# Two-layer hybrid step in split float32: three 256-column matmuls into one PSUM half instead of a 512- and a 256-column one

## The chip, the cores and the metric

The kernel runs on one core of a Trainium2 chip. The metric is the device time of one execution in microseconds; the median of several executions is compared. The engines are PE (TensorE, with its weight loads shown apart as PEld), DVE (VectorE), ACT (ScalarE), POOL (GpSimd) and SP (SyncE, which here only issues DMAs).

## The reference, cut to what matters

Two layers are computed for 128 context tokens and 128 latent tokens, 256 tokens in all. Nearly all of the arithmetic is in five products of a token matrix with a weight matrix, in each layer:

```
h = rms_norm(x, g_attn) * (1 + scale1) + shift1
proj = h @ w_in                                  # 2048 -> 3584
...                                              # conv module, two attentions -> concat
x = x + gate1 * (concat @ w_out)                 # 2048 -> 2048
h2 = rms_norm(x, g_mlp) * (1 + scale2) + shift2
x = x + gate2 * (square(relu(h2 @ w_mlp1)) @ w_mlp2)   # 2048 -> 8192 -> 2048
```

The modulation vectors (shift, scale, gate) come from a sixth product, silu(c) @ w_ada with 2048 x 12288 weights, for two vectors only. All inputs are float32, and nothing may be computed in a coarser format.

## The kernel before, in words

Tokens lie in the free dimension (256 columns, TOK), features in the partitions. Every weight matrix is walked in **pairs**: a pair is a strip of 512 output columns by 2048 rows, loaded by SP as four 1 MB blocks into `raw`. A layer has 2 + 3 + 2 pairs of w_in (kinds in1, in2, in3), 4 of w_out (out), and four chunks of 4 pairs of w_mlp1 (up) and 4 of w_mlp2 (down). That makes 43 pairs in a layer and 86 in the kernel.

To keep float32's accuracy each operand is split into two parts. ACT rounds a raw block into `hi` (L596) and DVE computes `lo` = raw - hi (L786), 1024 elements per partition at a time. The activations are kept split as well: `hs` (the normalized input) and `act2` (the mixer's output, or the hidden layer) hold for each of 16 feature tiles 512 columns, first the 256 of the high part and behind them the 256 of the low part. The product that is wanted is hi x high + hi x low + lo x high.

A pair has two groups g, and a group has 2 output tiles j with one PSUM bank each (banks 0 to 3 in all) and 16 steps k over the input features. For each (k, j), called a weight tile here, PE before the change issues two matmuls: L442 multiplies the hi tile with all 512 columns of the activations into the whole bank, so hi x high lands in the left half and hi x low in the right one, and L444 adds lo x high (256 columns) into the right half. There are 86 x 2 x 16 x 2 = 5504 weight tiles. Each matmul comes with a weight load of its own on PEld.

The two halves of a bank are added when it is read. ACT copies the right half into `tmp` (L642). DVE then adds left half and tmp. For in1 to in3 that sum goes to `zc` or `zq` (L839). For the others it goes to `tsum` (L842), and from there up squares the positive part (L845), and out and down add gate x sum to the residual `xT`, once for each stream of 128 tokens (L851). The semaphore `bank_freed` counts these adds, and PE waits for it before it starts on a bank again and at the start of attention. For out and down ACT squares the new residual (L653) and DVE adds it to `ssq` (L867), whose column sum PE needs for the next norm (L457).

Between the groups' own work DVE also does the 31 taps of the convolution (L884, 12 instructions behind each group of in2 and in3) and, in in3, the norms of queries and keys (reciprocals L921, product L927). PE does the modulation products (L380, L397) in between, as jobs of 4 units in a pair. Each engine takes its instructions in the written order: `walk` calls each engine's `pair` and `stage` in the same order, and the engines meet by semaphores only.

## Time and profile before

| | us |
|---|---|
| three timed executions | 2500.26, 2513.34, 2516.66 |
| their median | 2513.34 |
| span of the profiled execution, first to last instruction | 2495.1 |

The profiled execution has no time of its own beside its span. Its span lies 18.2 us under the median of the timed runs and 5.2 us under the fastest of them; what a timed execution has around the span is in that difference. Sums below are made on the span and moved to the median by adding 18.2. PE is the engine with the longest busy time.

### The profile page before, as it was taken

The page shows a single profiled execution, that of the slowest core. Times are in us where ns is not written, and L with a number is a line of the kernel's source. Part 1 is how long each engine was busy: PE and PEld are TensorE (multiplying, and loading weights), DVE is VectorE, ACT ScalarE, POOL GpSimd, SP SyncE. Part 2 cuts the span into 40 slices and gives each one's busy share as a digit, 9 for nine tenths or more (in the row PEclk, how much of TensorE's full clock was granted, in tenths as well). Part 3 has the DMA queues.
Part 4 walks back from the last instruction along what each step waited for, and adds up shares of the span by engine and source line. Part 5 has one row for each costly group of instructions (what it writes and reads, how often), then busy time and mean ns, then how long its engine had stood idle before and what let it go on. Part 6 is the DMA issues. An engine that isn't in the chain of part 4 may idle for free.

```text
span 2495.1 us, 41360 instructions
## 1 busy us (share of the span) xinstructions
PE 2326.7 (93%) x13464; PEld 1843.4 (74%) x13464; DVE 1541.3 (62%) x2642; ACT 1082.7 (43%) x1699; POOL 144.5 (6%) x196
## 2 busy tenths in 40 slices
PE   6699888979999999999997998797999999999997
PEld 2277556757887887787785775586778888888886
DVE  1357775574665565565567577867556666666666
ACT  1243334444444444444444333344444544545543
POOL 3101000001000001000100110000000000000000
PEclk9699899989999999999998998998999999999999
DMA  9878655858668768758854886444865655655662
GB/s 380 330 284 307 218 189 188 303 203 299 229 211 297 248 197 290 281 191 274 307 184 153 293 308 210 150 137 150 279 243 195 185 192 189 186 197 180 190 200 87
DMA packets 415092, 569.71 MB, mean 228 GB/s; under 512 B 9604, under 2 KB 364472, under 8 KB 414776
## 3 DMA queue, kind: packets, MB, share of 16 engines
q1 hardware_dynamic: 360504, 365.50, 44.8%
q0 software_dynamic: 52224, 201.34, 21.5%
q10 hardware_dynamic: 2304, 2.10, 0.2%
q8 instruction: 34, 0.56, 0.1%
q14 instruction: 26, 0.21, 0.0%
HBM read 565.76 MB, written 3.15 MB: 228 GB/s over the span
## 4 chain that ended last, share of the span: by engine, by line
PE 85%; DVE 6%; DMA 3%; ACT 2%; issue 2%; DVEq 1%; SPq 0%; ACTq 0%; POOL 0%; POOLq 0%
PE bank L442 51%; PE bank L444 25%; PE bank L380 6%; DMA ada<-in_w_ada 3%; PE bank L397 1%; DVE qrs L921 1%; DVE yconv L884 1%; PE bank L457 1%; DMA vrows<-in_g_final 1%; DVE lo L786 1%; DVE ybuf L1025 1%; DVE hs L1033 1%; DVEq L1033 0%; ACT prob L734 0%; ACT hs L754 0%
## 5 line engine op out<-in xcount | busy, mean ns | idle before, releaser
L442 PE MATMUL bank<-hs,hi 128*128 128x512 f32 x2944 | 1072.1, 407 | 49.0 <-DVE hs L1033 37.9
L786 DVE TENSOR_TENSOR lo<-raw,hi 128x1024 fp32r<-128x1024 f32 x685 | 816.9, 1223 | 453.6 <-ACT hi L596 453.2
L596 ACT ACTIVATE hi<-raw 128x1024 fp32r<-128x1024 f32 x685 | 704.0, 1055 | 575.0 <-PE bank L444 569.1
L442 PE MATMUL bank<-act,hi 128*128 128x512 f32 x2560 | 895.8, 396 | 6.0 <-DVE act L973 6.0
L444 PE MATMUL bank<-hs,lo 128*128 128x256 f32 x2944 | 827.4, 281 | 0.0
L442 PEld LDWEIGHTS bank<-hs,hi 128*128 128x128 f32 x2944 | 560.5, 190 | 295.4 <-issue 146.0
L444 PE MATMUL bank<-act,lo 128*128 128x256 f32 x2560 | 711.3, 278 | 0.0
L442 PEld LDWEIGHTS bank<-act,hi 128*128 128x128 f32 x2560 | 481.9, 188 | 131.2 <-issue 19.8
L444 PEld LDWEIGHTS bank<-hs,lo 128*128 128x128 f32 x2944 | 562.3, 191 | 1.4 <-issue 1.4
L444 PEld LDWEIGHTS bank<-act,lo 128*128 128x128 f32 x2560 | 482.6, 189 | 0.0
L642 ACT ACTIVATE tmp<-bank 128x256 f32<-128x256 f32 x344 | 113.4, 382 | 381.0 <-PE bank L444 381.0
L842 DVE TENSOR_TENSOR tsum<-bank,tmp 128x256 f32<-128x256 f32 x288 | 121.4, 422 | 200.0 <-ACT tmp L642 200.0
L349 POOL DMA_DIRECT2D ada<-in_w_ada x160 | 120.2, 751 | 1639.6 <-PE bank L380 1609.3
L380 PE MATMUL bank<-ada,cT 128*32 128x512 f32 x1344 | 184.7, 623 | 10.0 <-DMA ada<-in_w_ada 9.9
L653 ACT ACTIVATE thid<-xT 128x256 f32 (+1 forms) x160 | 67.1, 419 | 165.8 <-DVE xT L851 164.6
L851 DVE SCALAR_TENSOR_TENSOR xT<-tsum,mods,xT 128x128 f32 (+1 forms) x320 | 98.4, 349 | 43.1 <-DVE tsum L842 42.9
L884 DVE SCALAR_TENSOR_TENSOR yconv<-hpad,vecs,yconv 128x256 f32<-128x256 f32 x240 | 96.6, 479 | 0.0
L867 DVE TENSOR_TENSOR ssq<-ssq,thid 128x256 f32<-128x256 f32 x160 | 67.7, 423 | 31.4 <-ACT thid L653 31.2
L647 ACT ACTIVATE act<-thid 128x256 f32 x128 | 53.8, 420 | 73.7 <-DVE thid L845 73.7
L380 PEld LDWEIGHTS bank<-ada,cT 128*32 128x32 f32 x1344 | 27.0, 109 | 59.8 <-issue 40.2
L859 DVE TENSOR_TENSOR act<-thid,act 128x256 f32 x128 | 54.5, 426 | 25.9 <-ACT act L647 24.4
L397 PEld LDWEIGHTS bank<-cst,rows 128*128 128x128 f32 x384 | 52.9, 211 | 19.1 <-ACT rows L602 15.2
(127 smaller groups left out, 818.6 us busy)
## 6 DMA issues: line engine op xcount, KB each, us to landing
raw<-in_w_mlp SPq DMA_DIRECT2D x256, 1024.0 KB, 6.2
ada<-in_w_ada POOLq DMA_DIRECT2D x168, 1024.0 KB, 6.9
raw<-in_w_in SPq DMA_DIRECT2D x56, 1024.0 KB, 6.3
raw<-in_w_out SPq DMA_DIRECT2D x32, 1024.0 KB, 6.0
pre_a<-in_w_ada POOLq DMA_DIRECT2D x16, 1024.0 KB, 16.9
pre_q<-in_w_ada POOLq DMA_DIRECT2D x8, 1024.0 KB, 19.0
xtok<-in_x_prompt SPq DMA_DIRECT2D x1, 1024.0 KB, 11.9
xtok<-in_x_sample SPq DMA_DIRECT2D x1, 1024.0 KB, 21.3
```

Source lines behind the costliest of these rows:

```text
L349: pool.dma_start(ada[:, s % 2, :, :], src[:, 4 * s:4 * s + 4, bass.ds(b * 512, 512)]).then_inc(ada_landed[s % 2], 16)
L380: mm = pe.matmul(ada_ps[32 * q:32 * q + 32, :], cT[:, 4 * s + q, :], unit[:, q, :], start=(s == 0), stop=(s == 3))
L397: mm = pe.matmul(mod_ps[:, 2 * q:2 * q + 2], rows[:, q * P:(q + 1) * P], sel, start=True, stop=True)
L442: pe.matmul(bank[:, :], hi[:, h, k, j * P:(j + 1) * P], acts[:, k_, :], start=(k_ == 0), stop=False)
L444: mm = pe.matmul(bank[:, TOK:2 * TOK], lo[:, h, k, j * P:(j + 1) * P], acts[:, k_, 0:TOK], start=False, stop=(k_ == KT - 1))
L596: act.activation(hi[:, o % 4, :, :], raw[:, (o // 2) % 4, 4 * (o % 2):4 * (o % 2) + 4, :], ACT.Copy).then_inc(hi_ready, 1)
L642: act.activation(tmp[:, j, :], pb[2 * g + j][:, TOK:2 * TOK], ACT.Copy)\
L786: dve.tensor_tensor(lo[:, o % 4, :, :], raw[:, (o // 2) % 4, 4 * (o % 2):4 * (o % 2) + 4, :], hi[:, o % 4, :, :].bitcast(f32), ALU.subtrac ...
L842: dve.tensor_tensor(tsum[:, j, :], bank, tmp[:, j, :], ALU.add).then_inc(bank_freed, 1)
L851: dve.scalar_tensor_tensor(x, tsum[:, j:j + 1, s * P:(s + 1) * P], mods[:, l, bass.ds(gate + 4 * i + 2 * g + j, 1), s], x, ALU.mult, ALU.a ...
L867: dve.tensor_tensor(ssq[:, :], ssq[:, :], thid[:, j, :], ALU.add)\
L884: dve.scalar_tensor_tensor(y, hpad[:, ch, :, bass.ds(tap, P)], vecs[:, l, 1, bass.ds(4 * tap + ch, 1)], y, ALU.mult, ALU.add).then_inc(con ...
```

## The change: three matmuls per weight tile, and one half to read

The left half of the bank takes all three products, 256 columns each: hi x high, hi x low, lo x high. The number of columns that stream through PE for a weight tile stays 768. The number of matmuls and of weight loads goes from two to three, since the hi tile is named twice. Nothing is left in the right half.

The bank is then complete in one place. For in1 to in3 ACT copies it straight to `zc` or `zq`, and DVE has no part in it. For up ACT applies the relu on the way to `tmp` and DVE squares that. For out and down DVE reads the bank directly in the residual update and ACT has no part in it. `tsum` goes, and `bank_freed` and `x_updated` are replaced by three semaphores (`z_freed`, `hid_freed`, `res_freed`), each counted by the engine that reads. So that their counts can be constants, the loops over the out pairs and over the first chunk's up pairs are written out in the program, where they were loops on the engines' sequencers.

```diff
-                        after(pe, bank_freed, 4 * n + 2 * g - 2)
+                        if kind in ("out", "down"):
+                            after(pe, res_freed, res_tiles(l, c) + 4 * i + 2 * g - 2)
+                        if kind == "down":
+                            pe.wait_ge(hid_freed, up_tiles(l, c) + KT + 2 * g - 2)
+                        elif kind == "up":
+                            after(pe, hid_freed, up_tiles(l, c) + 4 * i + 2 * g - 2)
+                            pe.wait_ge(res_freed, res_tiles(l, c) + 2 * g - 2)
+                        elif kind != "out":
+                            after(pe, z_freed, in_tiles(l, kind) + 4 * (i - IN2 * (kind == "in3")) + 2 * g - 2)
...
-                                    pe.matmul(bank[:, :], hi[:, h, k, j * P:(j + 1) * P], acts[:, k_, :],
+                                    pe.matmul(bank[:, 0:TOK], hi[:, h, k, j * P:(j + 1) * P], acts[:, k_, 0:TOK],
                                               start=(k_ == 0), stop=False)
-                                    mm = pe.matmul(bank[:, TOK:2 * TOK], lo[:, h, k, j * P:(j + 1) * P],
+                                    pe.matmul(bank[:, 0:TOK], hi[:, h, k, j * P:(j + 1) * P], acts[:, k_, TOK:2 * TOK],
+                                              start=False, stop=False)
+                                    mm = pe.matmul(bank[:, 0:TOK], lo[:, h, k, j * P:(j + 1) * P],
                                                    acts[:, k_, 0:TOK], start=False, stop=(k_ == KT - 1))
...
                         for j in range(2):
-                            after(act, bank_freed, 4 * n + 2 * g + j - 1)
-                            act.activation(tmp[:, j, :], pb[2 * g + j][:, TOK:2 * TOK], ACT.Copy)\
-                               .then_inc(tmp_ready, 1)
+                            bank = pb[2 * g + j][:, 0:TOK]
+                            if kind in ("in1", "in2", "in3"):
+                                z = zc if kind == "in1" else zq
+                                act.activation(z[:, bass.ds(4 * i + 2 * g + j, 1), :], bank.unsqueeze(1), ACT.Copy)\
+                                   .then_inc(z_freed, 1)
+                            elif kind == "up":
+                                act.activation(tmp[:, j, :], bank, ACT.Relu).then_inc(hid_freed, 1)
...
-                            dve.wait_ge(tmp_ready, done)
-                            if kind in ("in1", "in2", "in3"):
-                                z = zc if kind == "in1" else zq
-                                dve.tensor_tensor(z[:, tile, :], bank.unsqueeze(1), tmp[:, j:j + 1, :], ALU.add)\
-                                   .then_inc(bank_freed, 1)
-                                continue
-                            dve.tensor_tensor(tsum[:, j, :], bank, tmp[:, j, :], ALU.add).then_inc(bank_freed, 1)
-                            dve.wait_ge(bank_freed, done)
+                            bank = pb[2 * g + j]
                             if kind == "up":
-                                dve.scalar_tensor_tensor(thid[:, j, :], tsum[:, j, :], 0.0, tsum[:, j, :],
-                                                         ALU.max, ALU.mult).then_inc(relu2_ready, 1)
-                            else:
+                                dve.wait_ge(hid_freed, up_tiles(l, c) + 4 * i + 2 * g + j + 1)
+                                dve.tensor_tensor(thid[:, j, :], tmp[:, j, :], tmp[:, j, :], ALU.mult)\
+                                   .then_inc(relu2_ready, 1)
+                            elif kind in ("out", "down"):
+                                dve.wait_ge(half_used, 8 * n + 4 * g + 4)
                                 gate = GATE1 if kind == "out" else GATE2
                                 for s in range(S):
                                     x = xT[:, tile, s * P:(s + 1) * P]
-                                    dve.scalar_tensor_tensor(
-                                        x, tsum[:, j:j + 1, s * P:(s + 1) * P],
+                                    update = dve.scalar_tensor_tensor(
+                                        x, bank[:, s * P:(s + 1) * P].unsqueeze(1),
                                         mods[:, l, bass.ds(gate + 4 * i + 2 * g + j, 1), s], x,
-                                        ALU.mult, ALU.add).then_inc(x_updated, 1)
+                                        ALU.mult, ALU.add)
+                                update.then_inc(res_freed, 1)
```

On PE the first pair of layer 0 (in1) begins like this before, in the program's order; hs, hi and lo are the operands named above:

```order
L457 MATMUL bank7<-ssq_65,ones_64 128x256 [waits ssq_set]
L442 MATMUL bank0<-hs_50,hi_53 128x512 [waits hs_ready,lo_ready]
L444 MATMUL bank0<-hs_50,lo_54 128x256
```

and like this after:

```order
L466 MATMUL bank7<-ssq_64,ones_63 128x256 [waits ssq_set]
L449 MATMUL bank0<-hs_50,hi_53 128x256 [waits hs_ready,lo_ready]
L451 MATMUL bank0<-hs_50,hi_53 128x256
L453 MATMUL bank0<-hs_50,lo_54 128x256
L449 MATMUL bank1<-hs_50,hi_53 128x256
```

One matmul has become two with the same weight tile, and all of a weight tile's three go to the same columns.

On DVE the first pair of in3 (layer 0) stands like this before:

```order
L786 TENSOR_TENSOR lo<-raw,hi 128x1024 [waits hi_ready] x4
L839 TENSOR_TENSOR zq<-bank,tmp 128x256 [waits tmp_ready] x2
L884 SCALAR_TENSOR_TENSOR yconv<-hpad,vecs,yconv 128x256 [waits conv_tap] x12
L921 RECIPROCAL qrs<-qrs 128x512 [waits qstd_ready] x2
```

and like this after:

```order
L799 TENSOR_TENSOR lo<-raw,hi 128x1024 [waits hi_ready] x4
L891 SCALAR_TENSOR_TENSOR yconv<-hpad,vecs,yconv 128x256 [waits conv_tap] x12
L928 RECIPROCAL qrs<-qrs 128x512 [waits qstd_ready] x2
```

The two adds between the splits and the convolution taps are gone, and with them DVE's wait for ACT's copy of the group that PE is still working on.

At the end of a group of out pairs DVE does this before:

```order
L842 TENSOR_TENSOR tsum<-bank,tmp 128x256 [waits tmp_ready]
L851 ISA [waits bank_freed]
L851 ISA
L851 SCALAR_TENSOR_TENSOR xT<-tsum,mods,xT 128x128
```

and this after:

```order
L857 SCALAR_TENSOR_TENSOR xT<-bank,mods,xT 128x128 [waits half_used]
L857 SCALAR_TENSOR_TENSOR xT<-bank,mods,xT 128x128
```

The update now waits for PE alone, and neither ACT's copy nor the sum stands ahead of it.

## Rows read from the trace of the kernel before

**Rows 1.** The page: span, and each engine's busy time, share and instructions.
```profile
span 2495.1 us, 41360 instructions
PE 2326.7 (93%) x13464; PEld 1843.4 (74%) x13464; DVE 1541.3 (62%) x2642; ACT 1082.7 (43%) x1699; POOL 144.5 (6%) x196
```

**Rows 2.** The page: the chain that ended last, by engine and by line.
```profile
PE 85%; DVE 6%; DMA 3%; ACT 2%; issue 2%; DVEq 1%; SPq 0%; ACTq 0%; POOL 0%; POOLq 0%
PE bank L442 51%; PE bank L444 25%; PE bank L380 6%; DMA ada<-in_w_ada 3%; PE bank L397 1%; DVE qrs L921 1%; DVE yconv L884 1%; PE bank L457 1%; DMA vrows<-in_g_final 1%; DVE lo L786 1%; DVE ybuf L1025 1%; DVE hs L1033 1%; DVEq L1033 0%; ACT prob L734 0%; ACT hs L754 0%
```

**Rows 3.** Busy time by windows: stretch, busy PE, PEld, DVE, ACT, POOL (instructions), clock, DMA.
```profile
1750.00:2475.00 725.00, 724.35 (x4192) 620.83 (x4192) 465.78 (x701) 349.10 (x507) 9.02 (x12) 1.00 0.60 197
```

**Rows 4.** Timeline of PE at full clock, out pair of layer 0: start, duration, instruction.
```profile
499.83 0.39 PE L442 MATMUL bank<-act,hi 128*128 128x512 f32 x1
500.06 0.27 PE L444 MATMUL bank<-act,lo 128*128 128x256 f32 x1
500.17 0.40 PE L442 MATMUL bank<-act,hi 128*128 128x512 f32 x1
...
500.52 0.39 PE L442 MATMUL bank<-act,hi 128*128 128x512 f32 x1
...
502.60 0.39 PE L442 MATMUL bank<-act,hi 128*128 128x512 f32 x1
```

**Rows 5.** Timeline of PEld, the same stretch.
```profile
500.06 0.19 PEld L442 LDWEIGHTS bank<-act,hi 128*128 128x128 f32 x1
500.17 0.19 PEld L444 LDWEIGHTS bank<-act,lo 128*128 128x128 f32 x1
```

**Rows 6.** The chain in order of time: eight matmuls summing in one bank, eight 2-column ones.
```profile
342.17 1.98 PE bank L457 x8
...
452.04 0.79 PE bank L397 x8
```

**Rows 7.** Timeline of PE at half clock (0.50), behind the third norm.
```profile
1347.00 0.63 PE L442 MATMUL bank<-hs,hi 128*128 128x512 f32 x1
1347.43 0.41 PE L444 MATMUL bank<-hs,lo 128*128 128x256 f32 x1
1347.64 0.63 PE L442 MATMUL bank<-hs,hi 128*128 128x512 f32 x1
```

**Rows 8.** Timeline of DVE in the first in3 pair, layer 0; brackets: idle before, and its releaser.
```profile
273.07 1.23 DVE L786 TENSOR_TENSOR lo<-raw,hi 128x1024 fp32r<-128x1024 f32 x1 [3.32 <-ACT hi L596]
276.87 0.76 DVE L839 TENSOR_TENSOR zq<-bank,tmp 128x256 f32<-128x256 f32 x2 [2.57 <-ACT tmp L642]
277.54 4.83 DVE L884 SCALAR_TENSOR_TENSOR yconv<-hpad,vecs,yconv 128x256 f32<-128x256 f32 x12
282.29 6.56 DVE L921 RECIPROCAL qrs<-qrs 128x512 f32<-128x512 f32 x2
288.76 4.56 DVE L786 TENSOR_TENSOR lo<-raw,hi 128x1024 fp32r<-128x1024 f32 x4
```

**Rows 9.** Timeline of ACT and PE, what that stretch waits for and holds up.
```profile
288.74 1.06 ACT L596 ACTIVATE hi<-raw 128x1024 fp32r<-128x1024 f32 x1 [2.19 <-PE bank L444]
...
302.37 2.08 PE L485 MATMUL bank<-zq,cst 128*128 128x512 f32 x2 [9.30 <-DVE zq L927]
```

**Rows 10.** Timeline of DVE at the entry of attention, layer 0.
```profile
330.20 4.62 DVE L786 TENSOR_TENSOR lo<-raw,hi 128x1024 fp32r<-128x1024 f32 x4
...
337.11 4.83 DVE L884 SCALAR_TENSOR_TENSOR yconv<-hpad,vecs,yconv 128x256 f32<-128x256 f32 x12
```

**Rows 11.** Timeline of ACT, DVE and PE at the end of the out pairs, layer 0.
```profile
508.29 0.66 ACT L642 ACTIVATE tmp<-bank 128x256 f32<-128x256 f32 x2 [2.48 <-PE bank L444]
509.39 0.61 DVE L851 SCALAR_TENSOR_TENSOR xT<-tsum,mods,xT 128x128 f32 x2 [0.26 <-DVE tsum L842]
511.79 0.43 DVE L867 TENSOR_TENSOR ssq<-ssq,thid 128x256 f32<-128x256 f32 x1 [0.24 <-ACT thid L653]
512.27 1.22 PE L457 MATMUL bank<-ssq,ones 128*128 128x256 f32 x2 [3.31 <-DVE ssq L867]
```

More of the change, by code:

```diff
@@ L48 @@
 PAIRS = DEPTH * PAIRS_LAYER
+Z_LAYER = 4 * (IN1 + IN2 + IN3)
 BANKS = 6 * D // 512
@@ L118, in build @@
     tmp = place("tmp", [P, 2, TOK], f32)
-    tsum = place("tsum", [P, 2, TOK], f32)
     thid = place("thid", [P, 2, TOK], f32)
@@ L194, in build @@
     half_used = sem("half_used")
-    tmp_ready = sem("tmp_ready")
-    bank_freed = sem("bank_freed")
+    z_freed, hid_freed, res_freed = sem("z_freed"), sem("hid_freed"), sem("res_freed")
     hs_ready = sem("hs_ready")
@@ L246, in walk @@
         stage("clear", -1)
-        with eng.Fori(0, OUT) as i:
+        for i in range(OUT):
             pair("out", n + i, i, -1, a + 16 + i if first else None, False)
@@ L250, in walk @@
         n += OUT
-        with eng.Fori(0, UP) as i:
+        for i in range(UP):
             pair("up", n + i, i, 0, a + 20 + i, False)
@@ L489, in attention @@
                     a = l * BANKS + (15 if l == 0 else 19)
-                    pe.wait_ge(bank_freed, 4 * (l * PAIRS_LAYER + IN1 + IN2 + IN3))
+                    pe.wait_ge(z_freed, Z_LAYER * (l + 1))
                     exchange(QW, 0)
@@ L650, in pair @@
                                 r = res_tiles(l, c) + 4 * i + 2 * g + j
-                                act.wait_ge(x_updated, 2 * r + 2)
+                                act.wait_ge(res_freed, r + 1)
                                 act.wait_ge(ssq_steps, ssq_base(l, c) + 4 * i + 2 * g + j)
@@ L669, in qk_norms @@
                         act.dma_start(ktokc[:, KV:2 * KV, :], t["cache_win_k"][0, l]).then_inc(cache_landed[0], 16)
-                        act.wait_ge(bank_freed, 4 * (l * PAIRS_LAYER + IN1 + IN2))
+                        act.wait_ge(z_freed, in_tiles(l, "in3"))
                         squares(l, 0)
@@ L764, in stage @@
                     elif name == "gate":
-                        act.wait_ge(bank_freed, 4 * (l * PAIRS_LAYER + IN1))
+                        act.wait_ge(z_freed, in_tiles(l, "in2"))
                         act.activation(zc[:, CT:2 * CT, :], zc[:, CT:2 * CT, :], ACT.Sigmoid)\
@@ L833, in pair @@
                             tile = bass.ds(4 * i + 2 * g + j, 1)
-                            done = 4 * n + 2 * g + j + 1
-                            bank = pb[2 * g + j][:, 0:TOK]
-                            dve.wait_ge(tmp_ready, done)
-                            if kind in ("in1", "in2", "in3"):
-                                z = zc if kind == "in1" else zq
-                                dve.tensor_tensor(z[:, tile, :], bank.unsqueeze(1), tmp[:, j:j + 1, :], ALU.add)\
-                                   .then_inc(bank_freed, 1)
-                                continue
-                            dve.tensor_tensor(tsum[:, j, :], bank, tmp[:, j, :], ALU.add).then_inc(bank_freed, 1)
-                            dve.wait_ge(bank_freed, done)
-                            if kind == "up":
-                                dve.scalar_tensor_tensor(thid[:, j, :], tsum[:, j, :], 0.0, tsum[:, j, :],
-                                                         ALU.max, ALU.mult).then_inc(relu2_ready, 1)
-                            else:
+                            bank = pb[2 * g + j]
+                            if kind == "up":
+                                dve.wait_ge(hid_freed, up_tiles(l, c) + 4 * i + 2 * g + j + 1)
[3 more added lines that the diff above has]
+                                dve.wait_ge(half_used, 8 * n + 4 * g + 4)
                                 gate = GATE1 if kind == "out" else GATE2
@@ L1077, in exps_before, with in_tiles @@
     return 5 * HEADS * l + 2 * min(e, HEADS) + 3 * max(0, e - HEADS)
+def in_tiles(l, kind):
+    return Z_LAYER * l + 4 * {"in1": 0, "in2": IN1, "in3": IN1 + IN2}[kind]
 def up_tiles(l, c):
```

2 lines of the change are left out of this document (1 added, 1 removed).

## The prediction

> **What bounds the kernel now.** I read the page first. PE is busy for 93% of the span, DVE for 62%, ACT for 43% [rows 1]. Busy shares of PE are modelled, so the chain of waits comes next: it runs on PE for 85% of the span, and 51% + 25% = 76% of the span lies on the two matmuls that the change touches, L442 and L444 [rows 2]. DVE has 6% of the chain, mostly around norms and attention. The windows say the same: in the up and down pairs of layer 1 PE is busy for 724.35 of 725.00 us at full clock [rows 3]. A cheaper evacuation on DVE or ACT gains nothing there. What counts is the time that PE takes for one weight tile, times 5504.
>
> That time is read from starts, since durations of successive matmuls overlap. In a steady stretch at full clock L442 starts at 499.83 and, eight weight tiles later, at 502.60 [rows 4]: 2.77 / 8 = 0.346 us for a weight tile. Within one, L444 starts 0.23 behind L442 (500.06 - 499.83), and the next L442 0.11 behind L444 (500.17 - 500.06). Over the eight tiles the second distance reads 0.11 or 0.12 alternately, so 0.115, and the first is what remains, 0.231. In columns that is 0.231 / 512 = 0.451 ns and 0.115 / 256 = 0.449 ns. Both shapes stream at the same price per column, with nothing left over for an instruction. At half clock a pair is 0.43 + 0.21 = 0.64 us for 768 columns [rows 7], again proportional, 0.83 ns per column.
>
> **The change, part by part.** (1) *Three matmuls for two, same columns.* The hi x high part is now 256 columns, hi x low 256 more, lo x high 256 as before. The row nearest to each of the three is L444 itself: a 256-column matmul with the next tile's 128-column load underneath, 0.115. So 3 x 0.115 = 0.345 against 0.346, which is -0.001 to -0.002 us for a tile; with -0.0015 x 5504 I take **-8 us**. The bounds come from the same rows. Below: all three at the lower reading, 3 x 0.1125 = 0.3375 (0.1125 because the view shows hundredths and reads 0.11), so -0.0085 x 5504 = -47 us. Above, first: all three at the higher reading, 3 x 0.1175 = 0.3525, so +0.0065 x 5504 = +36 us. The higher reading stands where the next matmul takes another row of the activations (k changes), and after the change the activations' address moves at nearly every matmul. Above, farther: see rival C.
>
> (2) *The third weight load.* A load has to fit under the matmul ahead of it. L442's load starts with L444 (500.06 both), L444's load with L442 (500.17 both) [rows 4, 5], and the matmul that uses L442's load starts 0.11 later, so a load needs at most 0.11 although its row says 0.19. That loads can follow each other at that rate is shown by the eight matmuls with only two moving columns each: 0.79 us, 0.10 each, or 0.11 if it is taken as seven distances [rows 6]. Loads are then 3 x 0.10 to 0.11 = 0.30 to 0.34 us of a tile's 0.345: hidden, with almost no room. Contention that lengthened a load would show at once, where today half of the loads have 0.23 us of cover. That counts for the upper side of the range. PEld's busy share would rise from 74% by about half, to some 110%; that is an artefact of overlapping records.
>
> The Trainium skill speaks against the change here: "TensorE: Matmul & The Clock Gate", The mechanism (Part 3), has weight loads overlap matmuls in flight only where the row groups differ, which they don't. By it each extra load, 0.10 us by the rows, would be exposed, 5504 x 0.10 = +550 us, time about 3050. The trace disagrees: the loads of rows 5 run under matmuls that use the same rows of the array. I give it 1 in 100. The same page, Back-to-back issue gap, adds a constant of about 2.5 ns to each warm matmul; by that one more matmul per tile would be 5504 x 2.5 ns = +14 us, an estimate. The rows show no constant, but can't exclude one so small.
>
> (3) *Adding to the same columns three times running.* Today the right half is written by two matmuls running. Eight matmuls of 256 columns into one bank's same columns take 1.98 us at attention's start, 0.25 each [rows 6]; these are slower plain float32 products, so it shows only that no large wait exists. I take zero, and the bound is the +36 above.
>
> (4) *Evacuation.* In steady pairs it lies beside PE and is worth nothing either way: a bank is wanted again a whole group, some 11 us, later (32 x 0.345). It counts where PE waits for DVE at the end. Three kinds of places:
>
> In in3 PE waits 9.30 us for the norms of queries and keys [rows 9], in each layer. DVE comes late to it because, behind its splits (end 273.07 + 1.23 = 274.30), it idles 2.57 us for ACT's tmp and adds for 0.76 before the taps can start at 277.54 [rows 8]. After the change the taps start at 274.3, the reciprocals end at 285.6 instead of 288.76, and the four splits follow. The last of these is then held by ACT's hi of 288.74 + 1.06 = 289.80 [rows 9], so it ends at 291.0 rather than 293.32: **2.3 us** are left of 3.2. Twice: 4.6.
>
> At the entry of attention the splits end at 330.20 + 4.62 = 334.82, yet the last taps start at 337.11 [rows 10] and PE's sum over the convolution follows them at 342.17 [rows 6]. Now nothing stands between: 2.3 us, twice, 4.6.
>
> At the end of out (two layers) and of the last down (two) the path is PE, tmp, tsum, xT, tsum, xT, thid, ssq, PE, from 508.29 to 512.27 = 3.98 us [rows 11]. After it, four updates at about 0.3 (0.61 for two), then square and add as before (0.43 each, with 0.1 between): 1.2 + 1.0 = 2.2. That is 1.8 less, four times: 7.2. It supposes that DVE reads PSUM in this operation as fast as SBUF.
>
> Together **-16 us**. If half of each turned into another wait it would be -8; nothing makes it a loss. ACT does the same number of reads or fewer, and its one new duty (zq itself) ends where tmp did.
>
> (5) *New waits and code.* PE's waits on z_freed, hid_freed and res_freed ask for reads a group back, long done. Behind a late one the whole PE stream would queue; I count zero. The out pairs and four up pairs of a layer are now straight code, and PE's program is longer; in3 is straight code already and its PE rows keep the pace between the waits. Zero, up to +10.
>
> **Sum.** 2495.1 - 8 - 16 = 2471 for the span, and with the 18.2 us between span and median 2489. That is 1.0% under 2513. A change under 1% either way can't be told from none in this kernel, whose three runs lie 0.65% apart.
>
> **The rivals.**
> A, *load-bound and faster*. The 512-column matmul has an excess of its own (0.231 against 0.213 for 512 columns at 2.4 GHz), and 256-column ones fall to the floor of the load, 0.1125. For it: half of the distances read 0.11 today. Against: the alternate ones read 0.12. -47 - 16 = -63: 2450.
> B, *each change of the activations' address costs*. 0.1175 for all three: +36 - 16 = +20: 2533. For it: the alternation of 0.11 and 0.12 goes with k. Against: 0.231 for 512 columns is twice 0.115, not twice 0.1175.
> C, *the excess belongs to the hi tile's matmul, not to its columns*; this is the case on the slow side. L442 takes 0.231 where 512 columns at 2.4 GHz are 0.213: 0.018 over. If that is a price of each matmul with a long-row hi operand, there are now two per tile: 2 x (0.107 + 0.018) + 0.115 = 0.365, +0.019 x 5504 = +105, less 16: 2602. It decides from an excess of 5 ns per tile up (5504 x 5 ns = 28 us, more than 16 + 8 together). For it: the excess is there at full clock and not at half clock, where 0.43 is 512 columns at 1.2 GHz. Against: per column both shapes agree to 0.5%.
> D, *the change doesn't do what it says*: a repeated load of the same tile is left out by the build. Then loads have more cover; columns still set the pace, and the time is the forecast's.
>
> **How the numbers follow.** Forecast with D 0.46 (2470 to 2505 by its own parts), A 0.20, B 0.18, C 0.13, anything else (exposed loads, new stalls) 0.03. The range 2448 to 2545 holds the forecast, A and B with the small constants, 0.84, and leaves out C. Faster by over 1% means under 2488: A whole and nearly half of the forecast's, 0.41. Within 1%: the rest of the forecast's and most of B, 0.42. Slower: C, a little of B, the rest, 0.17.
>
> **What the changed profile would show.** In a steady stretch, three matmul starts per tile at 0.11 to 0.12 and 0.345 in sum (0.3375 would be A, 0.3525 B, 0.365 C). PEld starts with each of them. PE's wait in in3 at about 7 us instead of 9.30; taps directly behind the splits there; 2.2 instead of 3.98 us from the last group to L457's successor. I am wrong if the tile's time is off by over 5 ns in either direction, since nothing else is multiplied by 5504.

## The result, and the profile after

| | before | after |
|---|---|---|
| median of four executions, us | 2514.04 | 2535.79 |
| their range | 2500.26 to 2516.66 | 2535.72 to 2537.56 |
| span of the profiled execution | 2495.1 | 2534.2 |

The ratio, taken over all executions of both, is 1.0098, with a 95% interval from 1.0067 to 1.0128: the change makes the kernel 1.0% slower. The medians lie 21.8 us apart, which is 0.9%. The forecast was 2489, a kernel faster by 1.0%. The measured time lies inside the stated range of 2448 to 2545, but the step went the other way. The profiled execution after took 2535.85 with a span of 2534.2, so only 1.65 us lie around a span. The executions before spread over 16 us, those after over 2 us; the profiled one before was a quick one, so the two spans lie 39.1 us apart where the medians lie 21.8 apart.

The page after, first the engines, then the chain of waits (to be compared with [rows 1, 2]):

```profile
span 2534.2 us, 50390 instructions
PE 2385.2 (94%) x18968; PEld 2162.0 (85%) x18968; DVE 1416.2 (56%) x2298; ACT 1036.3 (41%) x1539; POOL 144.5 (6%) x196
...
PE 87%; DVE 4%; DMA 3%; ACT 2%; issue 1%; DVEq 1%; SPq 0%; ACTq 0%; POOL 0%; POOLq 0%
PE bank L449 27%; PE bank L451 26%; PE bank L453 26%; PE bank L379 6%; DMA ada<-in_w_ada 3%; PE bank L396 1%; PE bank L466 1%; DVE hs L1040 1%; DMA vrows<-in_g_final 1%; DVE ybuf L1032 1%; DVE qrs L928 1%; DVEq L1040 0%; PE bank L494 0%; ACT prob L747 0%; SPq L311 0%
```

PE has 5504 more matmuls, DVE and ACT 344 and 160 fewer instructions. DVE's share of the chain fell from 6% to 4%, as an evacuation that got out of the way would make it. PE's share rose: 79% of a longer span lie on the three matmuls, 76% before. So the loss is to be looked for in the stream itself.

The timeline of PE in a steady stretch at full clock, up pair of layer 1 (start, duration, instruction), answers to [rows 4]:

```profile
1999.75 0.28 PE L449 MATMUL bank<-hs,hi 128*128 128x256 f32 x1
1999.87 0.28 PE L451 MATMUL bank<-hs,hi 128*128 128x256 f32 x1
1999.99 0.28 PE L453 MATMUL bank<-hs,lo 128*128 128x256 f32 x1
2000.11 0.28 PE L449 MATMUL bank<-hs,hi 128*128 128x256 f32 x1
...
2000.83 0.28 PE L449 MATMUL bank<-hs,hi 128*128 128x256 f32 x1
```

The durations of neighbours overlap, so the distances between starts are read. From 1999.75 to 2000.83 there are three weight tiles: 0.360 us for one, and each of the three matmuls takes 0.120. Before it was 0.346. The distance doesn't alternate any more, whether the activations' row changes or not. The windows say the same of a long stretch of layer 1 (columns as in [rows 3], which it answers to): 6023 / 3 = 2008 tiles in 725.00 us are 0.361 for one, where 4192 / 2 = 2096 were 0.346.

```profile
1780.00:2505.00 725.00, 725.00 (x6023) 713.00 (x6020) 406.75 (x561) 323.36 (x434) 8.27 (x11) 1.00 0.61 191
```

The loads start with the matmuls, 0.120 apart, by PEld's timeline (answers to [rows 5]):

```profile
1999.87 0.19 PEld L453 LDWEIGHTS bank<-hs,lo 128*128 128x128 f32 x1
1999.99 0.19 PEld L449 LDWEIGHTS bank<-hs,hi 128*128 128x128 f32 x1
2000.11 0.19 PEld L451 LDWEIGHTS bank<-hs,hi 128*128 128x128 f32 x1
```

At half clock, behind the third norm (window 1366.5 to 1369, granted clock 0.55 with its end at full), PE's timeline reads like this (answers to [rows 7]):

```profile
1366.35 0.41 PE L449 MATMUL bank<-hs,hi 128*128 128x256 f32 x1
1366.56 0.41 PE L451 MATMUL bank<-hs,hi 128*128 128x256 f32 x1
1366.78 0.41 PE L453 MATMUL bank<-hs,lo 128*128 128x256 f32 x1
1366.99 0.41 PE L449 MATMUL bank<-hs,hi 128*128 128x256 f32 x1
```

A tile takes 0.64 us there, exactly what two matmuls took before. 768 columns at 1.2 GHz are 0.640. So the third matmul costs 13.5 ns at full clock and nothing at half clock.

In sums over the whole trace: the distances from one matmul of a weight tile to the next such matmul (those under 0.7 us, so without waits) are 1934.9 us before and 1994.3 after, +59.4. This is called the stream below. All the rest, from PE's first start to its last, goes from 547.7 to 527.6, -20.1. Together that is +39.3, where the spans differ by 39.1. A tile at full clock takes 348.1 ns in the mean before and 359.8 after (some before run slower than 346.5, see experiment 8), and 11.7 ns for some 5040 of them is 59.

The second term is the evacuation, and it came as forecast. DVE, then PE, in the first in3 pair of layer 0 (answers to [rows 8, 9]):

```profile
275.66 1.23 DVE L799 TENSOR_TENSOR lo<-raw,hi 128x1024 fp32r<-128x1024 f32 x1 [3.35 <-ACT hi L605]
276.80 4.83 DVE L891 SCALAR_TENSOR_TENSOR yconv<-hpad,vecs,yconv 128x256 f32<-128x256 f32 x12
281.55 6.56 DVE L928 RECIPROCAL qrs<-qrs 128x512 f32<-128x512 f32 x2
288.02 3.43 DVE L799 TENSOR_TENSOR lo<-raw,hi 128x1024 fp32r<-128x1024 f32 x3
292.60 1.23 DVE L799 TENSOR_TENSOR lo<-raw,hi 128x1024 fp32r<-128x1024 f32 x1 [1.15 <-ACT hi L605]
```
```profile
302.88 2.08 PE L494 MATMUL bank<-zq,cst 128*128 128x512 f32 x2 [7.40 <-DVE zq L934]
```

The taps follow the split with nothing between, and PE waits 7.40 us instead of 9.30. The fourth split behind the reciprocals waits 1.15 us for ACT's hi, as the prediction supposed, and for longer. At attention's entry the splits end at 335.67, the taps run directly behind them, and PE's sum over yconv starts at 340.65 without a wait (answers to [rows 10]):

```profile
335.59 4.84 DVE L891 SCALAR_TENSOR_TENSOR yconv<-hpad,vecs,yconv 128x256 f32<-128x256 f32 x12
```
```profile
340.65 1.97 PE L466 MATMUL bank<-yconv,ones 128*128 128x256 f32 x8
```

And at the end of out, layer 0, four updates in 1.13 us, then the squares, and PE's wait is 1.40 instead of 3.31 (answers to [rows 11]):

```profile
510.15 1.13 DVE L857 SCALAR_TENSOR_TENSOR xT<-bank,mods,xT 128x128 f32<-128x128 f32 x4 [1.69 <-PE bank L453]
511.29 0.95 DVE L874 TENSOR_TENSOR ssq<-ssq,thid 128x256 f32<-128x256 f32 x2
```
```profile
512.30 0.70 PE L466 MATMUL bank<-ssq,ones 128*128 128x256 f32 x2 [1.40 <-DVE ssq L874]
```

### The profile page after: what moved, and what is told of

Same layout as the page of the kernel before. It is cut to its first block, busy times and chain, and to the rows that moved or that the text cites. A ratio compares the mean times of both kernels' runs of the same rounds, so it can differ in the third digit from the quotient of the medians.

```text
span 2534.2 us, 50390 instructions
## 1 busy us (share of the span) xinstructions
PE 2385.2 (94%) x18968; PEld 2162.0 (85%) x18968; DVE 1416.2 (56%) x2298; ACT 1036.3 (41%) x1539; POOL 144.5 (6%) x196
## 4 chain that ended last, share of the span: by engine, by line
PE 87%; DVE 4%; DMA 3%; ACT 2%; issue 1%; DVEq 1%; SPq 0%; ACTq 0%; POOL 0%; POOLq 0%
PE bank L449 27%; PE bank L451 26%; PE bank L453 26%; PE bank L379 6%; DMA ada<-in_w_ada 3%; PE bank L396 1%; PE bank L466 1%; DVE hs L1040 1%; DMA vrows<-in_g_final 1%; DVE ybuf L1032 1%; DVE qrs L928 1%; DVEq L1040 0%; PE bank L494 0%; ACT prob L747 0%; SPq L311 0%
## 5 line engine op out<-in xcount | busy, mean ns | idle before, releaser
L799 DVE TENSOR_TENSOR lo<-raw,hi 128x1024 fp32r<-128x1024 f32 x685 | 830.2, 1224 | 736.0 <-ACT hi L605 734.4
L605 ACT ACTIVATE hi<-raw 128x1024 fp32r<-128x1024 f32 x685 | 717.1, 1057 | 802.7 <-PE bank L453 795.3
L449 PE MATMUL bank<-hs,hi 128*128 128x256 f32 x2944 | 859.0, 292 | 46.0 <-DVE hs L1040 36.2
L451 PE MATMUL bank<-hs,hi 128*128 128x256 f32 x2944 | 838.7, 285 | 0.0
L449 PE MATMUL bank<-act,hi 128*128 128x256 f32 x2560 | 728.8, 285 | 5.4 <-DVE act L980 5.4
L451 PE MATMUL bank<-act,hi 128*128 128x256 f32 x2560 | 726.0, 284 | 0.0
L453 PE MATMUL bank<-act,lo 128*128 128x256 f32 x2560 | 725.9, 284 | 0.0
L449 PEld LDWEIGHTS bank<-hs,hi 128*128 128x128 f32 x2944 | 570.0, 194 | 164.4 <-issue 126.6
L451 PEld LDWEIGHTS bank<-hs,hi 128*128 128x128 f32 x2944 | 570.9, 194 | 1.4 <-issue 1.4
L449 PEld LDWEIGHTS bank<-act,hi 128*128 128x128 f32 x2560 | 493.0, 193 | 19.2 <-issue 10.9
L451 PEld LDWEIGHTS bank<-act,hi 128*128 128x128 f32 x2560 | 493.2, 193 | 0.0
L857 DVE SCALAR_TENSOR_TENSOR xT<-bank,mods,xT 128x128 f32 (+1 forms) x320 | 90.3, 345 | 75.8 <-PE bank L453 75.7
L850 DVE TENSOR_TENSOR thid<-tmp 128x256 f32<-128x256 f32 x128 | 48.8, 423 | 105.5 <-ACT tmp L656 105.4
L656 ACT ACTIVATE tmp<-bank 128x256 f32<-128x256 f32 x128 | 42.3, 383 | 151.1 <-PE bank L453 151.1
```

The costliest lines, as they stand in the source:

```text
L449: pe.matmul(bank[:, 0:TOK], hi[:, h, k, j * P:(j + 1) * P], acts[:, k_, 0:TOK], start=(k_ == 0), stop=False)
L451: pe.matmul(bank[:, 0:TOK], hi[:, h, k, j * P:(j + 1) * P], acts[:, k_, TOK:2 * TOK], start=False, stop=False)
L453: mm = pe.matmul(bank[:, 0:TOK], lo[:, h, k, j * P:(j + 1) * P], acts[:, k_, 0:TOK], start=False, stop=(k_ == KT - 1))
L605: act.activation(hi[:, o % 4, :, :], raw[:, (o // 2) % 4, 4 * (o % 2):4 * (o % 2) + 4, :], ACT.Copy).then_inc(hi_ready, 1)
L799: dve.tensor_tensor(lo[:, o % 4, :, :], raw[:, (o // 2) % 4, 4 * (o % 2):4 * (o % 2) + 4, :], hi[:, o % 4, :, :].bitcast(f32), ALU.subtrac ...
L850: dve.tensor_tensor(thid[:, j, :], tmp[:, j, :], tmp[:, j, :], ALU.mult)\
```

## The experiments

Each time is compared with executions of the kernel before that were measured beside it; their medians were 2517.42 (experiments 1 to 4), 2516.66 (5 and 8 to 10), 2517.18 (6, 7 and 11) and 2511.12 (12). The profile of the kernel before has a span of 2495.1, well under these. Experiments 2 to 8 with one execution each have no interval; they are there for their traces.

**The theory (P):** at full clock every matmul, with its own 128-column weight load, costs about 13 ns over its columns. Two made 320 + 26.5 = 346.5 ns before, three make 320 + 40 = 360. **The rivals:** (S) three products into the same PSUM columns hold each other up; (L) 0.120 is the time that a weight load needs, so that 256 columns no longer cover it; (R) it is a rate at which columns are taken, and more columns cost more of it; naming the same weight tile twice, or the order of the three, costs something; and, for the sum, that the evacuation lost time rather than gained it.

**1. Two halves.** The kernel before with L442 cut in two, each part into its own half. Evacuation as before.

```diff
-pe.matmul(bank[:, :], hi[...], acts[:, k_, :], start=(k_ == 0), stop=False)
+pe.matmul(bank[:, 0:TOK], hi[...], acts[:, k_, 0:TOK], start=(k_ == 0), stop=False)
+pe.matmul(bank[:, TOK:2 * TOK], hi[...], acts[:, k_, TOK:2 * TOK], start=False, stop=False)
```

> The kernel before, with only its 512-column matmul cut into two of 256 columns that write the two halves of the bank as before: three matmuls and three weight loads per weight tile, but evacuation, semaphores and loops of before. Theory P (a price of some 13 ns per matmul with its load, on top of its columns): 0.360 us per weight tile, as after the change, and a time some 58 us over the kernel before. Theory S (adding to the same 256 columns three times running is what costs): 0.346 us and no change. My prediction's cost per column alone: 0.346 and no change.

Measured 2553.36 (2553.07 to 2554.93); ratio to before 1.0145, interval 1.0128 to 1.0162. Timeline of PE:

```profile
1999.74 0.28 PE L442 MATMUL bank<-hs,hi 128*128 128x256 f32 x1
1999.86 0.28 PE L444 MATMUL bank<-hs,hi 128*128 128x256 f32 x1
1999.98 0.28 PE L446 MATMUL bank<-hs,lo 128*128 128x256 f32 x1
2000.10 0.28 PE L442 MATMUL bank<-hs,hi 128*128 128x256 f32 x1
```

Also 0.120 each and 0.360 for a tile, and the stream takes 1994.7 us where the change's takes 1994.3. Two halves or one makes no difference: S is out. The whole loss is there with the matmuls alone. What the change gets back by everything else, the evacuation above all, is 2553.36 - 2535.79 = 17.6 us; in the traces the rest of PE's time is 545.2 us here and 527.6 after the change, also 17.6. The expected 58 us came in the stream (+59.8 over the first profile), but in time the kernel is only 36 us over the executions beside it; experiment 8 shows why that can be.

**2. The lo matmul widened to 512 columns.** Still two matmuls, now 1024 columns; it adds lo x low, which isn't wanted.

```diff
-mm = pe.matmul(bank[:, TOK:2 * TOK], lo[...], acts[:, k_, 0:TOK], ...)
+mm = pe.matmul(bank[:, :], lo[...], acts[:, k_, :], ...)
```

> The kernel before, with the lo tile's matmul widened to all 512 columns (lo x high into the left half, lo x low into the right one, a term more than wanted): two matmuls, two loads, 1024 columns per weight tile. Theory P: 1024 columns at 2.4 GHz are 426.7 ns, plus 2 x 13.3 = 453 ns per weight tile, time about +590 us. Theory R (the price is one per column, 0.451 ns or 0.469 ns, and something shifts it from the lower to the higher): 462 or 480 ns, +636 or +735 us.

Measured 3061.24 in one execution, span 3059.5. Timeline of PE:

```profile
1999.63 0.39 PE L442 MATMUL bank<-act,hi 128*128 128x512 f32 x1
1999.85 0.39 PE L444 MATMUL bank<-act,lo 128*128 128x512 f32 x1
2000.08 0.39 PE L442 MATMUL bank<-act,hi 128*128 128x512 f32 x1
...
2000.99 0.39 PE L442 MATMUL bank<-act,hi 128*128 128x512 f32 x1
```

Three tiles in 1.36 us, 0.453 each: 1024 columns at 2.4 GHz are 426.7 ns, and 2 x 13.2 on top. In time it is 544 us over the 2517.42 beside it, less than the 590 that P had and farther from R's 636; the tile is what tells them apart. A price per column would give 1024 x 0.451 = 462 ns, and at the change's 0.120 for 256 columns 480: R is out. The price sits on the matmul (with its load), for 256 columns as for 512. L can't be the whole story either: under a matmul of 0.2265 us a load of 0.120 would not show, and the same 13 ns are there.

**3 and 4. Half of the lo load, and its control.** In both, the order is hi x high, lo x high, hi x low, so that the same hi tile is not named twice running; in 3 the lo matmul has 64 of its 128 weight columns and fills half of the output rows.

```diff
-pe.matmul(bank[:, 0:TOK], hi[...], acts[:, k_, TOK:2 * TOK], start=False, stop=False)
-mm = pe.matmul(bank[:, 0:TOK], lo[:, h, k, j * P:(j + 1) * P], acts[:, k_, 0:TOK], ...)
+pe.matmul(bank[0:64, 0:TOK], lo[:, h, k, j * P:j * P + 64], acts[:, k_, 0:TOK], ...)
+mm = pe.matmul(bank[:, 0:TOK], hi[...], acts[:, k_, TOK:2 * TOK], ...)
```

> The changed kernel with the order hi x high, lo x high, hi x low, and with the lo tile's load and matmul cut to 64 of 128 weight columns (the lo correction is left out for half of the outputs; the 256 streamed columns stay). Beside it e4_order has the same order with whole loads. Theory L (a load takes 0.120 us in this stream and 256 columns no longer cover it): the distance under which the halved load lies falls to 0.107 to 0.113, the other two stay at 0.120, some -0.01 per weight tile and -50 us. Theory P or R: all three stay at 0.120. If the price of 13 ns belongs to the load and goes with its columns: one distance 0.113.

> The changed kernel with the three matmuls in the order hi x high, lo x high, hi x low, so that no two neighbours use the same weight tile. Theory P, R and L: 0.360 us per weight tile and the changed kernel's time, 2536. If naming the same tile twice running had a price of its own: less than 0.360.

The control (all 128 columns) took 2537.53 with a span of 2535.9, 0.120 for each matmul and 0.360 for a tile:

```profile
1999.80 0.28 PE L453 MATMUL bank<-hs,hi 128*128 128x256 f32 x1
...
2000.16 0.28 PE L453 MATMUL bank<-hs,hi 128*128 128x256 f32 x1
```

So order and naming a tile twice cost nothing, and a repeated load isn't left out. With half of the lo load it is 2486.04, span 2484.3:

```profile
1999.76 0.28 PE L453 MATMUL bank<-hs,hi 128*128 128x256 f32 x1
1999.88 0.28 PE L449 MATMUL bank<-hs,hi 128*128 128x256 f32 x1
2000.00 0.28 PE L451 MATMUL bank<-hs,lo 128*64 128x256 f32 x1
2000.11 0.28 PE L453 MATMUL bank<-hs,hi 128*128 128x256 f32 x1
...
2001.16 0.28 PE L453 MATMUL bank<-hs,hi 128*128 128x256 f32 x1
```

Four tiles in 1.40, 0.350 each, so 10 ns of the 40 went with half a load: 51.5 us of 2537.5. No matmul lost a column of moving data. So in this form the excess goes with the weights (their load, or how many columns of the array they fill), not with the number of instructions alone. P as written down before the run had no change here and missed; L had the 50 us. A price in proportion to the width of the load would have given 6.7 ns, half of 13.3, so that isn't it either. The three distances read 116, 115 and 119 ns over the trace, where the expectation had all of them or two of them at 0.120; but distances between unequal neighbours don't say which matmul gained. This experiment alone does not exclude L.

**5. The lo matmul with 128 moving columns.** It leaves out the lo correction for the latent tokens. Its 53 ns of columns can't cover the load of the matmul behind it, so this shows what a load takes.

```diff
-mm = pe.matmul(bank[:, 0:TOK], lo[...], acts[:, k_, 0:TOK], ...)
+mm = pe.matmul(bank[:, 0:P], lo[...], acts[:, k_, 0:P], ...)
```

> The changed kernel with the lo tile's matmul cut to 128 of 256 columns (the lo correction is left out for the latent tokens), whole loads. Theory P with no floor under it: 640 columns at 2.4 GHz and 3 x 13.3 = 307 ns per weight tile, time about 2240. Theory P with a load's own time of 0.112 us (the 2-column matmuls) as floor: the distance behind the short matmul is 0.112, the tile 0.352, time about 2492. Theory L (a load takes 0.120 in this stream): that distance stays 0.120, the tile 0.360, time 2536.

Measured 2475.95, span 2474.2. A matmul that waits for its weights is recorded early here (0.33 instead of 0.28 long), so the loads are read. PEld:

```profile
1999.99 0.19 PEld L449 LDWEIGHTS bank<-hs,hi 128*128 128x128 f32 x1
2000.10 0.19 PEld L451 LDWEIGHTS bank<-hs,hi 128*128 128x128 f32 x1
2000.22 0.19 PEld L453 LDWEIGHTS bank<-hs,lo 128*128 128x128 f32 x1
2000.34 0.19 PEld L449 LDWEIGHTS bank<-hs,hi 128*128 128x128 f32 x1
```

L449's load starts with the short lo matmul, and the next load follows 0.11 later (0.108 to 0.112 over the trace); the two other distances are 0.116 to 0.125. So a load can be done in 0.11 in this stream. Together with experiment 2 that speaks against L: the 0.120 of the change is not a load laid bare, since a load would fit with 8 ns or more to spare. A tile takes 345 to 352 ns, 349 in the mean, against 352 expected by P with the load as a floor; the time is 16 us under the 2492 that went with it.

**6. Half of the rows.** The order of experiments 3 and 4, and the lo matmul with 64 of its 128 rows, to tell the load's columns from its rows (the line of hi x low moves behind it, not shown).

```diff
+pe.matmul(bank[:, 0:TOK], lo[0:64, h, k, j * P:(j + 1) * P], acts[0:64, k_, 0:TOK], ...)
```

> As e3_half_lo_load, but the lo tile is cut to 64 of its 128 rows (half of the contraction of lo x high is left out), with all 128 weight columns. If the price goes with weight columns: 0.360 per weight tile, 2537. If it goes with the amount loaded or with the rows in use: 0.350 and about 2486.

Measured 7466.22: nothing of the sort that was expected. PE, then PEld (the bracket is idle time before):

```profile
1999.79 0.41 PE L449 MATMUL bank<-hs,hi 128*128 128x256 f32 x1
2000.13 0.58 PE L451 MATMUL bank<-hs,lo 64*128 64x256 f32 x1
2000.64 0.58 PE L453 MATMUL bank<-hs,hi 128*128 128x256 f32 x1
2001.02 0.41 PE L449 MATMUL bank<-hs,hi 128*128 128x256 f32 x1
```
```profile
2000.13 0.28 PEld L451 LDWEIGHTS bank<-hs,lo 64*128 64x128 f32 x1 [0.22 <-issue]
2000.64 0.29 PEld L453 LDWEIGHTS bank<-hs,hi 128*128 128x128 f32 x1 [0.22 <-issue]
```

A tile takes 1.23 us, and the mean granted clock is 0.513, close to the lower of its two levels (1.2 of 2.4 GHz), though the timeline shows a matmul in flight all the time. Where the number of rows changes, PEld stands idle for 0.22 us and the load starts 0.34 and 0.51 us behind the start of the matmul ahead (1999.79 to 2000.13, 2000.13 to 2000.64); in the change it starts 0.003 behind it. The lower clock alone would make a tile of 0.64 us, by the rows behind the third norm, so some 0.59 us of the 1.23 come on top of it. This run says nothing on rows against columns; it shows a much larger price instead.

**7. The two-matmul form with half of the lo load.** The kernel before, lo ahead of hi (but at k = 0, where hi opens the bank), lo with 64 weight columns.

```diff
-pe.matmul(bank[:, :], hi[...], acts[:, k_, :], start=(k_ == 0), stop=False)
-mm = pe.matmul(bank[:, TOK:2 * TOK], lo[:, h, k, j * P:(j + 1) * P], ...)
+if k_ == 0:
+    pe.matmul(bank[:, :], hi[...], acts[:, k_, :], start=True, stop=False)
+pe.matmul(bank[0:64, TOK:2 * TOK], lo[:, h, k, j * P:j * P + 64], acts[:, k_, 0:TOK], ...)
+if k_ > 0:
+    mm = pe.matmul(bank[:, :], hi[...], acts[:, k_, :], start=False, stop=(k_ == KT - 1))
```

> The kernel before (512 and 256 columns, two halves), with the lo tile's load and matmul cut to 64 of 128 weight columns, as in e3_half_lo_load, and issued ahead of the hi tile's except at k = 0 (the lo correction is left out for half of the outputs). If the price of a matmul goes with the width of its load: about 10 ns per weight tile less than 0.346, as there, some -55 us. If the width told only because loads stood under every 256 columns: 0.346 and no change.

2484.24, span 2482.6. In the steady stretch a tile still takes 0.347 (three in 1.04):

```profile
2000.12 0.28 PE L445 MATMUL bank<-hs,lo 128*64 128x256 f32 x1
2000.24 0.39 PE L448 MATMUL bank<-hs,hi 128*128 128x512 f32 x1
...
2001.16 0.28 PE L445 MATMUL bank<-hs,lo 128*64 128x256 f32 x1
```

So the 10 ns of experiment 3 are not there at this place, and yet the execution is 12 to 21 us shorter in span than the two profiled ones before. Over the whole trace the mean tile at full clock is 347.7 ns, against 348.1 in the first profile, which is worth 2 us; where the other 10 come from was not found. I call this inconclusive: "so much for each column of a load" is not a law that the two forms share.

**8. The kernel before once more**, for the spread of its own executions.

> The kernel before, profiled a second time, to see what differs between its executions (2500 to 2518 us). If the price per matmul is fixed, its weight tiles take 0.346 us again and the difference sits in waits. If it depends on a state of the stream, more tiles than in the first profile take 0.360.

2505.17, span 2503.5, against 2495.1 for the same kernel in the first profile. Its stream of weight tiles takes 1944.0 us instead of 1934.9, which is all of the 8.4 us between the spans. Some stretches, nearly all beginning about 1 us behind modulation products and ending at the next ones, run at another pace:

```profile
571.17 0.40 PE L442 MATMUL bank<-hs,hi 128*128 128x512 f32 x1
571.41 0.28 PE L444 MATMUL bank<-hs,lo 128*128 128x256 f32 x1
571.53 0.40 PE L442 MATMUL bank<-hs,hi 128*128 128x512 f32 x1
```

0.24 + 0.12 = 0.36 for this tile, 0.35 for the next two: 353 in the mean of such a stretch instead of 346.5. Of some 5000 tiles at full clock 366 took 352 ns or more in the first profile, 763 in this one; as only one tile in three of a slow stretch is so long, they stand for three times as many. In the first profile each slow stretch is under 10 us long; here five of 86 to 91 us come to them, and 7 ns for each of their 1284 tiles are 8.7 of the 9.1 us. After the change, and in experiment 1, no such second pace is seen; there the executions agree within 2 us.

**9 to 12. Parts of the second term alone, on the kernel before.** Experiment 9 puts the convolution's taps ahead of the group's adds in in2 and in3. Experiment 10 also drops tmp and tsum for out and down: DVE updates the residual from the bank, left half, then right half. Experiment 11 writes out the loops over the out pairs and the first chunk's up pairs as the change does, and 12 is 9 and 11 together.

```diff
+if kind in ("in2", "in3"):              # 9, ahead of the adds; taken away behind them
+    for tap in range(TAPS_PAIR // 2):
+        conv_tap_ops(l, TAPS_PAIR * i + g * (TAPS_PAIR // 2) + tap + 1)
...
+for half in range(2):                   # 10, in place of L842 and L851
+    for s in range(S):
+        at_ = half * TOK + s * P
+        update = dve.scalar_tensor_tensor(x, pb[2 * g + j][:, at_:at_ + P].unsqueeze(1), mods[...], x,
+                                          ALU.mult, ALU.add)
...
-with eng.Fori(0, OUT) as i:             # 11, the same for the first Fori(0, UP)
+for i in range(OUT):
```

> The kernel before, with 512- and 256-column matmuls and two halves, and only DVE's order changed: in in2 and in3 the convolution taps stand ahead of the adds that read the bank, not behind them. If the waits for ACT's copy are what delayed DVE in in3 and at attention's entry: PE's wait in in3 falls from 9.3 to about 7 us, the entry shortens by 1 to 2 us, some -7 us in all. If the waits there are set by other work: no change.

> e7_taps_first, and in out and down DVE adds gate times the left half and gate times the right half straight from the bank to the residual, without ACT's copy and without the sum. From the last group to the column sum 8 updates of 0.3 and 1.0 us, 3.4 instead of 3.98 us, at four places: about -2 us against e7_taps_first, and no change in a weight tile's 0.346. If reading the bank on DVE were dearer than reading SBUF: longer than 3.98.

> The kernel before, with only the loops over the out pairs and the first chunk's up pairs written out, as the change does. My prediction counted zero, up to +10 us: the same time as before. If fetching straight code costs on PE: waits of PE's sequencer in those pairs and a time above 2525.

> The kernel before with two changes that touch no matmul: the convolution's taps ahead of the group's adds in in2 and in3, and the out pairs and the first chunk's up pairs written out. Each alone gave a ratio of 0.9975 and 0.9973 (about 6 to 7 us). If the two are independent, as the places are different (in3 and attention's entry, and the ends of out and up), the ratio is 0.995 (-12 us, 2500 to 2505). The rival is that each of the two verdicts was mostly the spread between executions of the two-matmul form, whose stream of weight tiles runs at 0.3465 us and in places at 0.353 us: then the two together give 0.997 to 0.998 once more, with spans between 2485 and 2505 by the number of tiles at the slower pace.

| experiment | median | ratio to before | 95% interval |
|---|---|---|---|
| 9, taps first | 2507.57 | 0.9975 | 0.9956 to 0.9995 |
| 10, and direct update | 2508.41 | 0.9976 | 0.9962 to 0.9991 |
| 11, written out | 2507.59 | 0.9973 | 0.9948 to 0.9997 |
| 12, 9 and 11 | 2506.60 | 0.9984 | 0.9964 to 1.0004 |

In 9 the distance from the last weight matmul to L485 in in3 falls from 9.575 to 7.77 us, as in the change (7.678). But at attention's entry it grows: from the last weight matmul to the sum over yconv it is 6.47 before and 8.67 and 8.74 here, where the last adds into zq now stand behind the taps. So the entry, expected to shorten by 1 to 2 us, gives the gain back. In 10 the four stage ends fall by 0.5, 0.6, 0.6 and 0.3 us, about as expected; read from the last weight matmul to the first column sum, 4.38, 4.58, 4.58 and 3.76 become 3.84, 3.95, 3.94 and 3.50. The median is no lower than in 9. In 11 nothing is lost by the longer program. But 9 and 11 do not add up: together they give 0.9984, the rival of that expectation, and its interval takes in no change. The traces say why: without the stream, PE's time is 547.4 us in 9, 545.8 in 11 and 547.1 in 12, against 547.7 and 546.8 in the two profiles of the kernel before; only 10, with 545.2, is a little lower. So outside the stream the profiled executions of 9, 11 and 12 show no gain beyond 2 us. The stream's pace differs from one execution to the next by more than that, and I do not claim a version that beats both kernels.

## Why the prediction was wrong

**Step (1), the price of the three matmuls, failed.** It took 3 x 0.115 = 0.345 for 0.346 and -8 us; the trace has 0.360 and +59.4 us. The wrong inference is the sentence "Both shapes stream at the same price per column, with nothing left over for an instruction". 0.231 and 0.115 are distances between unequal neighbours, and how they divide a tile does not say what each matmul costs. In experiment 2 the same 512-column matmul with an equal neighbour takes 0.2265, in experiment 1 the 256-column one 0.120. 0.2265 + 0.120 = 0.3465 gives back the tile of before. So the equality of 0.451 and 0.449 ns per column was an accident of where the start fell. The sum over a tile would have shown it: 346.5 - 320 = 26.5 ns over two matmuls. So would the half clock of [rows 7], where the same two take exactly their 640 ns of columns: a price in proportion to the columns would have been expected there as well, and it isn't there.

The Trainium skill says the same in kind: "TensorE: Matmul & The Clock Gate", Wait — 56ns, not 53.3ns?, has a fixed cost of each matmul that shows only at the full clock. The trace agrees in that (0.640 against 0.360), not in the size: the page has 2.5 ns, these runs 13.2 to 13.3 for a float32 matmul with its own 128-column load. The prediction weighed the rule at the page's 2.5 ns and missed that the rows held room for five times that.

**Step (2) held in part, step (3) held.** No load is laid bare: experiment 5 has a load at 0.11, and the +550 us of exposed loads did not come. But experiment 3 shows that a narrower load makes the tile shorter, which the step had at nothing as long as a load is hidden. Adding to the same columns three times costs nothing, by experiment 1.

**Step (4), the evacuation, held.** -16 was forecast; -17.6 is the difference between experiment 1 and the change, in time and in the traces. (The -20.1 against the first profile holds 2.5 us that experiment 1 has too, with the evacuation of before.) By places, from the last weight matmul on: in3 9.575 to 7.68 in both layers (-1.9 each, forecast -2.3); attention's entry, to the sum over yconv, 6.47 to 3.90 and 3.73 (-2.6 and -2.7, forecast -2.3 each); the four stage ends -1.9, -1.7, -2.1 and -1.3 (forecast -1.8 each). That is -16.1 together. The written-out loops are part of the 17.6 as well; experiment 11 puts them at 1 to 2 us in the trace, at most.

**Step (5), waits and code, held** on its lower side: nothing of the kind was lost (experiment 11).

**The base was off.** 18.2 us were added for what lies around a span. It is 1.65 us; the other 16.5 were that one execution's distance from the median. On its own time, 2495.1 + 1.65 + 59.4 - 20.1 = 2536.05 describes the profiled execution after (2535.85); the two terms are read from that trace, so this is an account and not a test. Against the median of before the change costs less, 21.8 us, since a usual execution of before has a longer stream (experiment 8: +9.1 us in an execution of 2505). That the whole way to 2514 is the same was not shown; no execution of the kernel before as long as that was profiled. With the base right, step (1) as forecast would have given some 2473 for an execution like the profiled one.

**The rivals.** B gave 2533, by the number nearly right, but by luck: its +36 for the stream is 23 us short of the +59.4, and a base 16.5 us too high and 4 us less taken off for the evacuation make up for nearly all of that. Its mechanism isn't there: each of the three matmuls takes 0.120, whether the address changes or not. The mechanism is nearest to C's, an excess of the matmul rather than of its columns, at 13.5 ns per tile instead of 19: 0.360 instead of 0.365. C had it on the hi tile's matmuls alone; all three have it. C had the right reading of the half clock among its grounds, and was given 0.13. Its point from which the change loses, 5 ns per tile, was passed by far. D is excluded by the 18968 loads and by experiment 4.

**What stays open:** where in the hardware the 13 ns arise. Experiment 3 shows that they shrink with the width of the weights, experiments 2 and 5 that they are not a load laid bare, experiment 6 could not tell columns from rows, and experiment 7 doesn't fit a simple rule. No run has a matmul without a load of its own, so the price of the matmul and that of its hidden load are not told apart. A form that keeps two matmuls and yet fills one half, by an output pattern that names 256 columns twice, was not tried.

## What to carry to other kernels

To price one more matmul, add up a whole repeating unit of the stream, take off its columns at the granted clock level, and divide the rest by the number of matmuls; don't divide the distance from one start to the next. Look for the same unit at the lower clock level: an excess that is gone there, as here, speaks for the instruction or its load and against the columns. And add to a span only what one execution's own time has around it; the rest of the way to the median is spread, which can be larger than the effect that is forecast.

## What the runs showed of the hardware that was not expected

- At full clock a float32 matmul with a 128-column load costs 13.2 to 13.3 ns beyond its columns (0.1200 for 256 in experiment 1, 0.2265 for 512 in experiment 2), at half clock nothing (0.640 for 768).
- A matmul of 64 rows between two of 128 makes a tile take 1.23 us instead of 0.36, at a mean granted clock of 0.51 (experiment 6). The lower clock alone makes 0.64 of it, as seen behind the third norm. What holds the clock down was not found.
- The alternation of 512- and 256-column matmuls has a second pace, 353 instead of 346.5 ns for a tile, in stretches that differ from one execution to the next; five long ones explain 8.7 of the 9.1 us between the two streams of the kernel before. There the excess is 33 ns for two matmuls instead of 26.5. What sets it off is not known.
- PE's busy share rose from 93% to 94% and PEld's from 74% to 85% (110% was forecast): neither says how near a stream is to its limit.
